# Context rows of the last layer's scans carry only the state; window attention alternates score places and lags by one unit more

## What is computed

```python
def bidir(step, init, ctx_f, lat_f, ctx_b, lat_b):
    flip = lambda seqs: tuple(jnp.flip(a, 2) for a in seqs)
    hc_f, st_f = chunked_scan(step, init, ctx_f)
    hl_f, _ = chunked_scan(step, st_f, lat_f)
    hc_b, st_b = chunked_scan(step, init, flip(ctx_b))
    hl_b, _ = chunked_scan(step, st_b, flip(lat_b))
    return hl_f + jnp.flip(hl_b, 2), hc_f + jnp.flip(hc_b, 2)

# window_gqa: a block of 128 queries reads the 3 key blocks around it (band of 128 each way),
# and all context keys, and a sink logit joins the softmax
    s_loc = jnp.einsum('bnqhgd,bnkhd->bnhgqk', qb, kw).astype(F32) * scale
    s_loc = jnp.where(valid[None, :, None, None], s_loc, -jnp.inf)
    s_ctx = jnp.einsum('bnqhgd,bchd->bnhgqc', qb, kc).astype(F32) * scale
    p = jax.nn.softmax(jnp.concatenate([s_loc, s_ctx, sink], axis=-1), axis=-1)

# reference: with_ctx = l < DEPTH - 1, so the last layer's context outputs are dropped,
# while the state that the context rows leave behind still starts the latent scans
```

## Time and profile before

| | |
|---|---|
| runs | 2335.21 us median, 2332.82 to 2339.88 |
| profiled execution | 2340.97 us, its span 2339.2 us |
| mean granted TensorE clock | 0.929 of full |
| last layer's mLSTM scan | about 1372 to 1448 us |
| last layer's GLA scan | about 1532 to 1634 us |
| window attention, layer 0 and 1 | 854 to 948 us, 2030 to 2116 us |

### The profile page before, as it was taken

How to read it: one execution, slowest core, us unless ns; L and a number is a source line. 1 busy time by engine, 2 the same in 40 slices (tenths; PEclk the granted TensorE clock), 3 DMA queues, 4 the chain that set the end, 5 groups by cost and what they waited for, 6 DMA issues and landing times. The chain is left out here.

```text
span 2339.2 us, 37578 instructions
## 1 busy us (share of the span) xinstructions
PE 1982.7 (85%) x14664; PEld 1644.9 (70%) x14664; DVE 1354.3 (58%) x2545; ACT 985.9 (42%) x2076; POOL 500.5 (21%) x642
## 2 busy tenths in 40 slices
PE   5889889897777868898987988988987778688988
PEld 3778778786665647787866877877876566577767
DVE  5156428778878367222765356268578782672257
ACT  5243332336868436311224333322358684262121
POOL 2203325311010100322214124244120101002212
PEclk8899999998989979999998999998989898799999
DMA  9840350240000410313239601600420004102231
GB/s 397 294 139 2 96 158 2 58 124 1 1 1 1 140 41 1 91 58 125 113 124 337 197 27 46 182 27 5 116 62 1 1 1 131 49 2 72 72 127 54
DMA packets 69614, 203.25 MB, mean 87 GB/s; under 512 B 8096, under 2 KB 11456, under 8 KB 65984
## 3 DMA queue, kind: packets, MB, share of 16 engines
q0 software_dynamic: 38016, 93.34, 14.0%
q1 hardware_dynamic: 26240, 98.08, 11.6%
q10 hardware_dynamic: 5184, 9.44, 1.1%
HBM read 180.83 MB, written 19.92 MB: 86 GB/s over the span
## 5 line engine op out<-in xcount | busy, mean ns | idle before, releaser
L774 PE MATMUL ps<-ring_lo,h_hi 128*128 128x512 f32 (+3 forms) x800 | 271.5, 340 | 0.0
L774 PE MATMUL ps<-h_hi,ring_lo 128*128 128x512 f32 (+1 forms) x688 | 251.0, 365 | 0.0
L2375 DVE TENSOR_REDUCE a_st<-ps 128x1 f32<-128x1280 f32 (+1 forms) x144 | 196.7, 1369 | 42.7 <-PE ps L2260 42.2
L2328 ACT ACTIVATE ring<-ps,a_st 128x1280 f32<-128x1280 f32 (+1 forms) x144 | 177.4, 1232 | 54.7 <-DVE a_st L2375 54.4
L2260 PE MATMUL ps<-a_k,a_q 128*128 128x512 f32 (+1 forms) x400 | 126.7, 427 | 53.1 <-ACT ring L2328 48.7
L774 PEld LDWEIGHTS ps<-ring_lo,h_hi 128*128 128x128 f32 x800 | 158.7, 198 | 13.6 <-issue 0.5
L774 PE MATMUL ps<-h_hi,g_proj_wh 128*128 128x512 f32 (+1 forms) x400 | 148.9, 372 | 12.1 <-DVE ring_lo L732 7.2
L774 PE MATMUL ps<-g_proj_xl,g_proj_wh 128*128 128x512 f32 (+1 forms) x400 | 148.3, 371 | 0.0
L774 PEld LDWEIGHTS ps<-h_hi,ring_lo 128*128 128x128 f32 x688 | 130.3, 189 | 21.3
L2277 PE MATMUL ps<-cst,ring 128*128 128x128 f32 x656 | 107.2, 296 | 42.2 <-ACT ring L2337 16.3
L2260 PEld LDWEIGHTS ps<-a_k,a_q 128*128 128x128 f32 x400 | 73.8, 213 | 82.0 <-ACT ring L2328 65.7
(11 more groups left out here) (379 smaller groups left out, 5258.5 us busy)
## 6 DMA issues: line engine op xcount, KB each, us to landing
ring<-in_w SPq DMA_DIRECT2D x14, 2048.0 KB, 7.5
a_proj_xl<-h_low POOLq DMA_DIRECT2D x64, 320.0 KB, 3.2
ring<-in_w SPq DMA_DIRECT2D x32, 512.0 KB, 3.8
b_proj_xl<-h_low POOLq DMA_DIRECT2D x22, 640.0 KB, 4.4
d_proj_xl<-h_low POOLq DMA_DIRECT2D x32, 320.0 KB, 3.2
h_low<-h_low SPq DMA_DIRECT2D x32, 256.0 KB, 4.1
yT<-in_w SPq DMA_DIRECT2D x16, 512.0 KB, 7.2
g_proj_xl<-h_low POOLq DMA_DIRECT2D x32, 256.0 KB, 5.5
```

The costliest lines, as they stand in the source:

```text
L774: last = pe.matmul(out, left, right, start=k == 0 and (p, q) == self.HIGH[0], stop=k == KT - 1 and (p, q) == self.LOW[0])
L2328: act.activation(p(u, c, n), ps[:, 3 * c:3 * c + 3, :].rearrange("p b n -> p (b n)")[:, 0:n], ACT.Exp, bias=st[:, 0:1], accum_out=st[:, 1: ...
L2375: dve.tensor_reduce(stat[:, u % SLOTS, c, 0:1], ps[:, 3 * c:3 * c + 3, :].rearrange("p b n -> p (b n)")[:, 0:n], AX.X, ALU.max, negate=Tru ...
```

## The change

`silent(env)` is 4 in the last layer and 0 in the first; D is that number. For units below D the mLSTM scan keeps only `fresh`, the scaling of the values and the state update; `logs` and `scores` of unit D stand ahead of the loop. The GLA scan keeps of them `fresh`, two of the eight decay columns (four matmuls of 128 columns, an exponential of 128x256), the keys' token scaling and the state update. The counts in the waits are shifted by D.

In window attention of both layers the scores are split into a near part (up to three tiles, masks first, now one matmul for each head over the whole near width) and a context part. Head 0 keeps its places, head 1 alternates between banks 2-3 and banks 3-4, so the near part of a unit may be written while the last unit's exponentials are still to come; only the context part waits for both. Transposes lag by two units (they were one behind), values by three (they were two), `p` has three buffers, the fifth tile's transposes and the output share bank 7, and VectorE takes `shifts(u)` ahead of `norm(u-1)`.

```diff
+def silent(env):
+    return sum(tile < NC for _, _, tile in UNITS) if env["last"] else 0
...
@@ mLSTM scan, TensorE (D = silent(env))
-                logs(0)
-                scores(0)
+                logs(D)
+                scores(D)
                 for u, (way, i, j) in enumerate(UNITS):
-                    if u + 1 < NU:
+                    if D < u + 1 < NU:
                         logs(u + 1)
...
                     for h in range(HEADS):
                         last = pe.matmul(fresh_of(u)[half(h), h // 2, :], ktm[:, j, h * DH:(h + 1) * DH],
                                          vw[:, u % 2, h, :], start=True, stop=True)
+                    if u < D:
+                        last.then_inc(u_mm.sem, 1)
+                        continue
...
@@ mLSTM scan, VectorE
+                def finish(u):
+                    way, i, j = UNITS[u]
+                    dve.wait_ge(u_mm.sem, u + 1)
+                    if u < D:
+                        new_state(u)
+                        return
...
@@ GLA scan, GpSimd
+                    if u < D:
+                        pool.tensor_tensor(kx[:, u % 2, 0, :], decays[u % 2][:, 0, :], k_tok[:, UNITS[u][2], :], ALU.mult)\
+                            .then_inc(k_scaled.sem, 2)
+                        continue
@@ GLA scan, ScalarE
-                    act.activation(decays[u % 2][:, :, :], ps[:, 4:6, :].rearrange("p b (n t) -> p (b n) t", n=4), ACT.Exp)\
+                    used = slice(0, 8, 7 if u < D else 1)
+                    act.activation(decays[u % 2][:, used, :], ps[:, 4:6, :].rearrange("p b (n t) -> p (b n) t", n=4)[:, used, :], ACT.Exp)\
@@ GLA scan, TensorE
+                    if u < D:
+                        whole = sums[:, way, 7 * P:8 * P]
+                        pe.matmul(ps[:, 5, 3 * P:BANK], la_hi[:, j, at], whole, start=True, stop=False)
+                        pe.matmul(ps[:, 5, 3 * P:BANK], la_lo[:, j, at], whole, start=False, stop=True).then_inc(expo_mm.sem, 1)
+                        return
...
                 for u in range(NU):
-                    levels(u)
+                    if u >= D:
+                        levels(u)
                     fresh(u)
                     if u + 2 < NU:
                         exponents(u + 2)
-                    if u >= 1:
+                    if u >= D + 1:
                         out(u - 1)
@@ GLA scan, VectorE
+                    if u < D:
+                        pass
+                    elif second_visit(u):
                         dv2.mark(dve.tensor_tensor(hC[:, j, :, :], o, hC[:, j, :, :], ALU.add))
...
@@ window attention
+        def context_first(u, kv):
+            return kv == 1 and u % 2 == 1
...
+        def near_place(u, kv):
+            n = len(near_tiles(u)) * P
+            return (4, slice(0, n)) if context_first(u, kv) else (2 * kv, slice(BANK - n, BANK))
+
+        def context_place(u, kv):
+            return (3, slice(BANK - NC * P, BANK)) if context_first(u, kv) else (2 * kv + 1, slice(0, NC * P))
+
+        TURN, FIFTH, OUT = 5, 7, slice(2 * P, 3 * P)
...
-            p = tile("p", [P, 2, KV, 5 * P])
+            p = tile("p", [P, 3, KV, 5 * P])
...
@@ window attention, GpSimd
-                pool.tensor_copy(band[:, :, :], C(env, "band").rearrange("p (a b) -> p a b", a=2)).then_inc(masks.sem, 1)
                 pool.tensor_copy(same[:, :], C(env, "ident")).then_inc(masks.sem, 1)
+                pool.memset(band[:, P:2 * P].bitcast(F32), 0.0).then_inc(masks.sem, 1)
+                for side in range(2):
+                    pool.tensor_copy(band[:, 2 * side * P:(2 * side + 1) * P], C(env, "band")[:, side * P:(side + 1) * P]).then_inc(masks.sem, 1)
@@ window attention, TensorE
+                def mask(u, kv):
...
+                    pe.matmul(ps[:, bank, at], same[:, :], band[:, c:c + len(near) * P], start=True, stop=False, skip_group_check=True)
...
                 def scores(u):
...
+                    if near:
+                        if u >= 2:
+                            pe.wait_ge(exped.sem, KV * (u - 1))
+                        mask(u, 1)
+                        if u >= 1:
+                            pe.wait_ge(exped.sem, KV * (u - 1) + 1)
+                        mask(u, 0)
+                        products(u, near[0], near[-1] + 1, near_place, False)
                     if u >= 1:
                         pe.wait_ge(exped.sem, KV * u)
+                    products(u, 0, NC, context_place, True).then_inc(s_mm.sem, 1)
...
                 for u in range(NU):
                     scores(u)
-                    if u >= 1:
-                        turns(u - 1)
                     if u >= 2:
-                        value(u - 2)
+                        turns(u - 2)
+                    if u >= 3:
+                        value(u - 3)
+                turns(NU - 2)
+                value(NU - 3)
                 turns(NU - 1)
...
@@ window attention, ScalarE
                     if n > 4:
                         act.wait_ge(t_mm.sem, before(u) + 3)
+                        if u >= 1:
+                            act.wait_ge(o_kept.sem, u)
...
-                    if u >= 1:
-                        keep(u - 1)
+                    if u >= 2:
+                        keep(u - 2)
+                keep(NU - 2)
                 keep(NU - 1)
@@ window attention, VectorE
                 for u in range(NU):
+                    shifts(u)
                     if u >= 1:
                         norm(u - 1)
-                    shifts(u)
-                    if u >= 2:
-                        keep_out(u - 2)
+                    if u >= 3:
+                        keep_out(u - 3)
```

More of the change, by code:

```diff
@@ L2476, in _, with products @@
             @block.tensor
             def _(pe):
+                def mask(u, kv):
+                    near = near_tiles(u)
+                    bank, at = near_place(u, kv)
+                    c = (near[0] - pairs[u][0] + 1) * P
+                    pe.matmul(ps[:, bank, at], same[:, :], band[:, c:c + len(near) * P], start=True, stop=False, skip_group_check=True)
+                def products(u, k0, k1, place, start):
+                    t, g = pairs[u]
+                    for kv in range(KV):
+                        bank, at = place(u, kv)
+                        last = pe.matmul(ps[:, bank, at], qkT[rows(kv), g, t * P:(t + 1) * P], qkT[rows(kv), 2, k0 * P:k1 * P],
+                                         start=start, stop=True, tile_position=(64 * kv, 0), skip_group_check=True)
+                    return last
@@ L2493, in scores @@
-                    for kv in range(KV):
-                        for n, m in masked:
-                            last = pe.matmul(ps[:, 2 * kv + n // 4, n % 4 * P:(n % 4 + 1) * P], same[:, :], band[:, m, :],
-                                             start=False, stop=True, skip_group_check=True)
-                    last.then_inc(s_mm.sem, 1)
+                    products(u, 0, NC, context_place, True).then_inc(s_mm.sem, 1)
                 def turns(u):
-                    n = width(u) // P
+                    n = tiles(u)
@@ L2518, in value @@
                         pe.wait_ge(o_kept.sem, u)
-                    for n, (k, _) in enumerate(kt):
+                    for n in range(tiles(u)):
                         for kv in range(KV):
-                            last = pe.matmul(ps[rows(kv), 7, 0:P], vD[:, k, rows(kv)], aT[:, u % 2, kv, n, :],
-                                             start=n == 0, stop=n == len(kt) - 1, tile_position=(0, 64 * kv))
+                            last = pe.matmul(ps[rows(kv), FIFTH, OUT], vD[:, key_tiles(u, kv)[n], rows(kv)], aT[:, u % 2, kv, n, :],
+                                             start=n == 0, stop=n == tiles(u) - 1, tile_position=(0, 64 * kv), skip_group_check=True)
                     last.then_inc(o_mm.sem, 1)
```

169 lines of the change are left out of this document (89 added, 80 removed).

## The result

Faster, by 0.9%. The changed kernel took 2317.34 us (median of 7 runs, 2307.62 to 2323.55) beside 2335.70 us for the kernel before (7 runs, 2332.82 to 2339.88): ratio 0.9909, 95% interval 0.9888 to 0.9929. The same pair, compared again on another chip, gave 2306.94 beside 2338.57, ratio 0.9863 (0.9838 to 0.9888). The forecast of 2302 from 2335.21 is a ratio of 0.9858. The sign and the profiled pair (2340.97 to 2309.04, -31.9 us against -33.2 forecast) came out; the first median lies 2.3 us above the range of 2290 to 2315, the second inside it.

A forecast was written before the change was run, and what follows sets the result against it. No single bound: VectorE's work set a GLA unit, TensorE never rested between mLSTM units, a score-exponential ring set window units. -11.3 - 11.4 - 10.5 = -33.2 us, 2340.97 to 2307.8, less 5.8 above median: 2302, range 2290 to 2315.

The forecast's parts named there:

- Bound and ring: Window attention: scores, maxima, second head's exponential, next scores set the 4.91 us unit; opened, TensorE's issue becomes the bound.
- the old issue of 4.06 and one gap of 0.33: Inner window unit: TensorE's issue time plus one idle gap ahead of the transposes, 4.4 us, saving 0.5.
- (3): Rival, window stage: wide masks and fewer, wider products bring the unit to 4.1 us; 2296 in all, chance 0.08.
- (2): Rival, window stage: second 0.33 us gap and three waits keep the unit about 4.9 us; 2313 in all, chance 0.12.
- mLSTM: Last layer's scan: four context units keep only state work, first five units 17.2 to 5.6 us; -11.3, bounds -9.6 and -12.2.
- GLA: Last layer's scan: first `levels` come earlier, at 10.8 us after stage start; -11.4 us, bounds -8 and -15.
- the 13 that I had called fatal: GLA scan: first `levels` later than 13 us after the stage's first instruction would make the forecast wrong.
- two units are in flight, so 1.2 each: GLA start: a context unit's chain of some 2.3 us overlaps with another's, costing 1.2 us per unit.
- the 3.4 + 0.9 that I put there: GLA scan, taken off the saving: 3.4 us of pipeline filling that stays, 0.9 for narrow matmuls at half clock.
- Window: Both layers' window attention: inner units and first rounds gain, masks and longer tail cost; -5.2 a layer, -10.5 both.
- Rival (1), the clock: GLA start: thinner context units leave whole units at half clock, 9 us lost, 2311; chance 0.12. Counterargument: VectorE sets units.
- the runs themselves spread over 7 us: Run-to-run spread of the whole kernel, used with term errors of 3 (scans) and 5 (window) to set the range.

The follow-up runs named there:

- e6: Changed kernel with one score place in every unit and scores again waiting for both exponentials of the unit before, longer lags kept; 2325.58 us, 0.9950.
- e9: Changed kernel with the window lags of the kernel before and TensorE's value products ahead of the transposes; 2309.93 us, 0.9888.
- e8: Changed kernel with unread products filling TensorE's idle stretches at the start of both layers' GLA scans; 2301.04 us, 0.9858.
- e1: Kernel before with only the last layer's two scans changed, window attention old; 2319.19 us, 0.9913.
- e4: Kernel before, run again with no edit for a second trace; 2336.56 us, 0.9992.
- e5: Changed kernel with TensorE's one wait ahead of the window transposes split by bank, the fifth tile's copy awaited last; 2305.79 us, 0.9868.
- e11: Changed kernel with the old window lags, alternating score places kept, plus unread products at the start of both GLA scans; 2295.28 us, 0.9824.
- e12: e11 with the wait ahead of the window transposes split by bank as in e5; 2300.76 us, 0.9839.

## Why the prediction was right, and where it was not

**Bound and ring: right, the unit by two errors.** e6 puts the wait for the exponential back, and the unit with it (4.86). The unit was forecast as 4.4 and measured as 4.32 to 4.38. But I had it as the old issue of 4.06 and one gap of 0.33. The weight loads of a unit now take 0.30 + 0.95 + 0.86 + 0.25 + 1.07 = 3.43 us, and there are four gaps, 0.25, 0.33, 0.17 and 0.17, 0.92 together: 4.35. The old unit had 3.9 of loads, the gap of 0.17 and one of 0.12 between its 128-wide score products and its masks, too short to be printed (2058.06 + 1.17 to 2059.35): the reading "no such gap" was not quite right. So both rivals were half right, (3) with cheaper masks and products, 0.4 less, and (2) with gaps ahead of the masks and behind them, 0.4 more, and they cancel. The gaps stand where one tiling gives way to another and are missing between two full-array groups (e9). At 1.2 GHz the gap behind the 256-wide products is 0.65 us, twice as long, with nothing awaited (changed kernel, layer 1):

```profile
2005.05 0.29 PEld L2550 LDWEIGHTS ps<-d_band,d_same 128*128 128x128 f32 x1 [0.65 <-issue]
```

The rule of the Trainium skill (TensorEngine Tiling (Array Packing), Key Properties), that a change of tiling mode drains the engine, agrees, and should have been counted at each change.

**mLSTM: right.** Forecast -11.3, measured -10.7 in the profiled pair and -11.4 between the two kernels again; first set to next unit 2.27 us against 2.4.

**GLA: the sum right by luck, two of its steps wrong.** -11.4 was forecast and -11.4 measured in the profiled pair (101.0 to 89.6). But the first `levels` came at 12.75 us, not 10.8, just short of the 13 that I had called fatal. The step that failed is "two units are in flight, so 1.2 each": exponents have one pair of banks, so a unit of context costs 1.65 us at half clock (1.35 at full, e8), and unit 4's exponents with their hand-over 2.4 us (1520.71 + 0.38 to 1523.53), not 1.4. The other error hid this: the filling behind it cost less than the 3.4 + 0.9 that I put there. Unit 4's `levels` moved by 26.59 - 12.75 = 13.8 us against the earlier trace rows, the stage shrank by 11.4, so 2.5 were lost. And the worth itself is not a constant. The four executions with the old code in this stage (101.0, 93.8, 98.0, 98.0) have a mean of 97.7, the seven with the new code and no added products one of 88.0: -9.7 rather than -11.4. The profiled pair set an execution of the old code with much time at 1.2 GHz (18.8 us) beside one of the new code with much (28.2 us), and came out at the forecast; the two kernels again give 6.5 (93.8 to 87.2).

**Window: right in sum, sizes off.** Forecast -5.2 a layer; measured -4.8 and -6.8 in the profiled pair. In layer 1: start +0.4 (forecast +0.5), first three units -3.7 (forecast -3.0 for the first rounds), ten inner units -5.8 (forecast -5.0), edges -0.2 (-0.4), tail +2.5 (+2.7). The steps between first row maxima were 5.28, 6.13 and 5.40 us and are 4.39, 4.92 and 3.76: a round of 3.7 was forecast from the first on and comes only with the third. The first layer, which I took as equal, came 0.4 short, the last 1.6 beyond.

**Rival (1), the clock: partly true.** In the last layer's GLA start TensorE ran at 1.2 GHz for some 20 us ((1 - 0.64) / 0.5 x 13 + 11), and the unread products show that the half clock is worth 4.7 us on average (88.0 to 83.3). The new scan is at 1.2 GHz for 23.2 us on average where the old was for 11.6: that fits what this rival said of thinner context units, but the ranges overlap (13.7 to 28.4 against 0.0 to 18.8), so that the change brought it is likely and not shown. At the same 13.7 us the new code would have gained 12.7 (98.0 to 85.3) and not 9.7, so the clock took back some 3 us (an estimate) of the 9 that the rival feared. My argument against it, that VectorE sets a GLA unit and does not slow, is wrong at 1.2 GHz: a unit then takes 7.3 us (e9) against 4.4, with TensorE busy 27.22 of 28 us. So a prolonged half clock costs 3 us a unit, twice what the rival reckoned. The first layer's scan, which the change left alone, took 91.5 to 103.4 us to its last pick, with 3.4 to 37.5 us of the scan at 1.2 GHz. The Trainium skill (TensorE: Matmul & The Clock Gate, Part 1) says that the same kernel warms up at different points from run to run, and the traces agree, inside the kernel too.

**The median.** The term that failed is the spread: "the runs themselves spread over 7 us". That came from three runs of the kernel before; 23 runs of it on the chip of e1 to e4 spread over 23 us. The seven runs of the first comparison spread over 16 us, and the mean granted clock goes with them, 0.926 at 2307.62 and 0.916 at 2323.55. If half clock is the cause, 0.010 of the span is 46 us more at 1.2 GHz, for 16 us of time. The changed kernel is also granted less than the kernel before: 0.916 to 0.928 in its thirteen runs, against 0.919 to 0.937 in those 23. The profiled one was near the best (2309.04), so where the others lost their time was not seen; e9's profile and the table of the GLA scans show one place where such a loss arises. Why the first comparison gave -18.4 and the second -31.6 stays open to that extent.

## What to carry to other kernels

When leading units of a pipeline lose most of their work, price the chain that remains by its buffers (here one pair of banks: exponents, exponential, exponents), not by the number of units in flight. When a ring is opened by a second place for its data, try that alone first; longer lags only pay if something still waits, and their price is a longer tail. A start-up stretch made thinner can give back part of what was saved through the clock (here some 3 of 12.7 us, an estimate from single profiles): look at the granted clock there in more than one execution, and try unread products. When one stage varies between profiles, compare executions with equal time at the lower clock before reading a gain off a pair.

## What the runs showed of the hardware

- A weight load that follows tiled products, the last of them 256 columns wide, in another tiling starts 0.33 us late at 2.4 GHz and 0.65 at 1.2 GHz. One behind 128-column value products or transposes starts 0.17 late, one from 384-column masks to 64-row tiles 0.25; between two full-array groups there is none (changed kernel, e9). The profile may put a releaser's name to such a gap: it named a copy on which the 0.33 us do not hang (e5, e6, e9), and "issue" where nothing was awaited.
- With sixteen unread products in the last layer and eight in the first the granted clock was 1.00 through the first 21 us of the last layer's GLA scan (e8, e11, e12), and that scan was 4.7 us shorter on average; in e8 it fell again near the end (6.5 us at 1.2 GHz).
- In the last layer's GLA scan 18.8 us at 1.2 GHz go with 7.2 us more of the old code (93.8 to 101.0), 28.4 us with 7.3 more of the new (82.5, with the products, to 89.8).
- TensorE was busy 27.22 of 28 us and was still granted 1.2 GHz throughout (e9).
